# Expert weights stored in HBM in the order in which they are loaded

## The reference

```python
def expert_choice_ffn(x, router_w, wg, wu, wd):
    cap = CAPACITY_FACTOR * n // N_EXPERTS            # 32 tokens for each of 16 experts
    aff = softmax(einsum('bnd,de->bne', x, router_w))
    gate, idx = lax.top_k(aff.transpose(0, 2, 1), cap)
    xg = x[bidx, idx]
    hid = silu(einsum('becd,edf->becf', xg, wg)) * einsum('becd,edf->becf', xg, wu)
    o = einsum('becf,efd->becd', hid, wd) * gate[..., None]
    return zeros_like(x).at[bidx, idx].add(o)
```

## Time and profile before

| | |
|---|---|
| median of three runs | 2715.48 us (2713.36 to 2717.77) |
| span of the profiled execution | 2717.3 us |
| TensorE busy, granted clock (mean) | 2302.9 us (85%), 0.965 |
| VectorE, ScalarE busy | 1037.0 us (38%), 811.7 us (30%) |
| DMA | 660.17 MB, 243 GB/s over the span |
| chain that ended last | PE 57%, DMA 29%, DVE 7%, ACT 4% |

### The profile page before, as it was taken

One profiled execution on the slowest core, in us unless ns is written; L12 is line 12 of the kernel. 1 busy time (PEld: TensorE's weight loads), 2 busy tenths in 40 slices (PEclk: granted clock), 3 DMA queues, 4 the chain that ended last, 5 costly groups with the idle time before them and its releaser, 6 DMA issues.

```text
span 2717.3 us, 32508 instructions
## 1 busy us (share of the span) xinstructions
PE 2302.9 (85%) x13952; PEld 1613.8 (59%) x13952; DVE 1037.0 (38%) x1361; ACT 811.7 (30%) x989; POOL 67.6 (2%) x99
## 2 busy tenths in 40 slices
PE   5998888777777898787777778999999989988997
PEld 3855643222222585631111116999899989988997
DVE  4536451000000455510000004556855555556555
ACT  3425321000000344410000004432744354434433
POOL 0022000000000002000000000000000000000000
PEclk8999899999999998899999999999999999999998
DMA  7392357999999330389999995554355444452542
GB/s 264 109 385 107 120 220 280 409 409 410 410 410 410 143 131 6 118 323 409 409 410 410 410 410 204 179 180 175 123 186 186 167 149 165 181 186 93 186 165 72
DMA packets 205376, 660.17 MB, mean 243 GB/s; under 512 B 5632, under 2 KB 27136, under 8 KB 198624
## 3 DMA queue, kind: packets, MB, share of 16 engines
q1 hardware_dynamic: 204176, 653.67, 62.6%
q0 software_dynamic: 1104, 5.11, 0.5%
HBM read 657.71 MB, written 1.05 MB: 242 GB/s over the span
## 4 chain that ended last, share of the span: by engine, by line
PE 57%; DMA 29%; DVE 7%; ACT 4%; SPq 2%; issue 1%; POOL 0%; DVEq 0%; ACTq 0%; POOLq 0%
PE ps L694 13%; PE ps L695 13%; PE ps L696 13%; DMA ring<-in_exp_up 13%; DMA ring<-in_exp_gate 11%; PE ps L1011 6%; DMA ring<-in_w_in 2%; DVE ring_r L361 2%; PE ps L567 2%; SPq L453 2%; DMA ring<-in_ffn_gate 2%; ACT ring_r L354 1%; PE ps L833 1%; PE ps L1026 1%; PE ps L723 1%
## 5 line engine op out<-in xcount | busy, mean ns | idle before, releaser
L1011 PE MATMUL ps<-ring,arena 128*64 128x512 f32 (+1 forms) x2048 | 466.6, 600 | 165.1 <-DMA ring<-in_exp_up 81.9
L694 PE MATMUL ps<-h_buf_r,ring_r 128*128 128x256 f32 (+1 forms) x1856 | 540.8, 291 | 17.6 <-DVE h_buf_r L652 12.2
L696 PE MATMUL ps<-h_buf_r,ring_r 128*128 128x256 f32 (+1 forms) x1856 | 537.9, 290 | 0.0
L361 DVE TENSOR_TENSOR ring_r<-ring,ring_r 128x4096 fp32r<-128x4096 f32 (+2 forms) x97 | 406.2, 4192 | 304.6 <-ACT ring_r L354 304.6
L695 PE MATMUL ps<-h_buf_r,ring_r 128*128 128x256 f32 x1696 | 482.9, 285 | 0.0
L1011 PEld LDWEIGHTS ps<-ring,arena 128*64 128x64 f32 (+1 forms) x2048 | 128.2, 124 | 502.2 <-issue 295.3
L354 ACT ACTIVATE ring_r<-ring 128x4096 fp32r<-128x4096 f32 (+2 forms) x97 | 332.7, 3434 | 262.4 <-DMA ring<-in_ffn_down 107.6
L694 PEld LDWEIGHTS ps<-h_buf_r,ring_r 128*128 128x128 f32 x1856 | 360.4, 194 | 22.9 <-issue 16.7
L696 PEld LDWEIGHTS ps<-h_buf_r,ring_r 128*128 128x128 f32 x1856 | 360.2, 194 | 3.3
L695 PEld LDWEIGHTS ps<-h_buf_r,ring_r 128*128 128x128 f32 x1696 | 328.8, 194 | 0.2
L695 PE MATMUL ps<-arena_r,ring_r 128*128 128x256 f32 (+1 forms) x944 | 278.3, 295 | 0.0
(11 more groups left out here) (273 smaller groups left out, 2325.0 us busy)
## 6 DMA issues: line engine op xcount, KB each, us to landing
ring<-in_exp_gate SPq DMA_DIRECT2D x64, 2048.0 KB, 23.7
ring<-in_exp_up SPq DMA_DIRECT2D x64, 2048.0 KB, 23.8
ring<-in_exp_down SPq DMA_DIRECT2D x64, 2048.0 KB, 23.7
ring<-in_ada_w SPq DMA_DIRECT2D x24, 2048.0 KB, 14.7
ring<-in_ffn_gate SPq DMA_DIRECT2D x20, 2048.0 KB, 7.7
ring<-in_ffn_up SPq DMA_DIRECT2D x20, 2048.0 KB, 7.8
ring<-in_ffn_down SPq DMA_DIRECT2D x20, 2048.0 KB, 7.9
ring<-in_w_in SPq DMA_DIRECT2D x6, 2048.0 KB, 20.8
```

Of the source, the lines that this page charges most:

```text
L361: dve.tensor_tensor(rest, slot(n)[:, 0:halved[n]], lead, ALU.subtract).then_inc(sem("chunk_halved"), 1)
L694: release(pe.matmul(out, a[0], b[0], start=start, stop=False, skip_group_check=True))
L696: return pe.matmul(out, a[1], b[0], start=False, stop=stop, skip_group_check=True)
L1011: mm = pe.matmul(ps[half * m:half * m + m, which, :], xe[:, k, :], slot(n + c)[:, D * (k % 4) + 512 * half:D * (k % 4) + 512 * half + 512] ...
```

## The change

The host stores the three expert arrays as (layer, expert, half, partition, 4096 floats). One load is then one stretch of 2 MB in HBM and one partition's part of it one row of 16 KB. The load on SyncE becomes a plain copy of [128 x 4096]. The bytes that land in each partition of the slot, the number of loads, their order, their waits and all that reads the slots stay as they are.

```diff
@@ -449,8 +449,8 @@
                         sp.wait_ge(weights_used, it * 24 + (n + c - SLOTS + 1))
                         half = c % 2
-                        src = w[l, it * 4 + c // 6, half * 512:half * 512 + 512, :].rearrange("(k p) n -> p k n", p=P)
-                        sp.dma_start(slot(n + c).rearrange("p (k n) -> p k n", k=4), src)\
+                        src = w[l, it * 4 + c // 6, half, :, :]
+                        sp.dma_start(slot(n + c), src)\
                             .then_inc(slot_loaded[slot_of[n + c]], 16)
@@ -2310,6 +2310,10 @@
+    def by_partition(w):
+
+        return w.reshape(LAYERS, EXPERTS, 2, 4, P, -1).transpose(0, 1, 2, 4, 3, 5).reshape(LAYERS, EXPERTS, 2, P, SLOT)
+
@@ -2330,7 +2334,8 @@
-        "exp_gate": a["exp_w_gate"], "exp_up": a["exp_w_up"], "exp_down": a["exp_w_down"],
+        "exp_gate": by_partition(a["exp_w_gate"]), "exp_up": by_partition(a["exp_w_up"]),
+        "exp_down": by_partition(a["exp_w_down"]),
```

## The result

The kernel with the change ran at a median of **2676.7 us** (2671.1 to 2678.1, 4 runs) against 2716.1 us (2713.4 to 2717.8, 4 runs) for the kernel before: 39.4 us less, ratio 0.9849, 95% interval 0.9835 to 0.9863. The forecast was 2676 us, a range of 2669 to 2690.

The account below looks back on a forecast made before the run. DMA transfers were taken to bound the two expert stages, the only ones at a DMA limit. 180 loads at 0.22 us less each give 39.5 us, so the median 2715.5 us becomes 2676 us, range 2669 to 2690.

Parts of the forecast that it names:

- What bounds the kernel: Two expert stages: DMA transfers at 410 GB/s set the end of both; PE follows, needing 22.96 us an expert against 30.7.
- Which loads count: Expert stages: 90 of 96 loads in each layer, 180 in all; the first six are hidden behind the router.
- The prediction's check: Layer 0: first landing at 435.5 us plus 90 loads of 5.12 us plus one w_in load gives 901.7, against 903.3 us.
- What a load costs: Each expert load: 4.90 us with 16 KB rows against 5.12 now, 0.22 us less; 39.5 us in 180 loads.
- The straight line: Row price under a full queue: 150.9 ns per 4096 bytes plus 9.1 ns a row, so 612.7 ns at 16 KB.
- The rule of about 3 cycles a packet: Other price for expert loads' rows: an estimated 3.5 ns fixed overhead per packet, giving 15 us saved, not 39.5.
- The other parts of the edit: SyncE's issue, PE's chain between gate, up and down, instruction fetches and other engines' work: no cost found.
- landing near 22.8 us: Sign in the profile after: an expert load mid-stage takes near 22.8 us from issue to landing, against 23.8 before.
- Rows are not cut: Expert loads: the rival had 16 KB rows cut into 4 KB pieces at issue, nothing changing, 2715 us; chance 6%.
- Only a third of the price: Expert loads: rival that only a third of the 9.1 ns a row goes, 13 us saved, 2702 us; chance 4%.
- The place in HBM gives the gain: Expert loads: rival that most of the rate difference comes from where rows lie, not a fixed row price; 2702 us, chance 4%.
- The spacing slows HBM: Expert stages: rival that rows starting at multiples of 16 KB clash in memory, 54 us more, 2769 us; chance 5%.

Follow-up runs that it names:

- e1: The changed kernel with each partition's part of a load fetched as two rows of 8 KB instead of one of 16 KB; 2688.0 us, before 2717.3.
- e2: The changed kernel with each partition's part of a load fetched as eight rows of 2 KB; 2771.9 us, ratio 1.0207 to the kernel before.
- e3: The changed kernel with each partition's four 4 KB pieces one behind the other in HBM, 512-byte gaps keeping them separate rows; 2716.2 us, before 2717.3.
- e8: The kernel with the change run again, unaltered, beside other experiments; 2675.3 us, ratio 0.9850 to the kernel before.
- e4: The changed kernel with the 16 KB rows of a load 512 KB apart instead of adjacent; 2677.1 us, ratio 0.9855 to the kernel before.
- e10: The changed kernel with the 16 KB rows of a load 1 MB apart; 2671.7 us, ratio 0.9836 to the kernel before.
- e5: The changed kernel with all three expert arrays in one, the 16 KB rows of a load 4 MB apart; 3414.4 us, ratio 1.257 to the kernel before.

## Why the prediction was right, point by point

**What bounds the kernel** was read rightly, shown by e1, e2 and the change: a price of so many ns on each row moved the whole time by some 180 times what it did to a load, in both directions. What the reading of the chain left out is SyncE's held issue, 1.6% of it; e1 shows that it was no cost of its own.

**Which loads count**: 90 in each layer. By the measured rows a load takes 32 x 160.0 ns before and 8 x 612.0 ns after, 0.224 us less; 90 times that is 20.2 us, and the stretches in the table shrank by 20.2 and 20.3. All 96 would have given 21.5. The lengths alone don't settle it: e3, with rows of 4 KB, has stages of 482.2 and 477.4 us, 0.8 and 1.5 us more than before. What does is the DMA engines between PE's first expert matmul and the seventh load: 3 GB/s in both profiles (421.8 to 428 us before, 417.9 to 424 after), so the first six loads had landed and nothing waited for them.

The prediction's check, 901.7 us for w_in against 903.3, came so close by luck: 435.5 us is already the landing of the first of the 90, so 89 loads follow it, and the sum is 896.6. That is 6.7 us short, and counted the same way from 431.1 us the kernel after is 6.5 us short (872.6 for 879.1), so the gain is not touched.

**What a load costs.** Sum 39.5 us, stages 40.5 in the profiles, medians 39.4 in the first comparison and 41.4 in e8's. The term was a hair small: 612.0 ns and not 612.7. (The printed 160.0 ns would give 39.3 us; 39.5 comes from the unrounded 160.04.) That the median came within 0.7 us of 2676 is partly luck, since runs of one kernel spread over 4 to 7 us. The straight line was the right choice between the bounds of 27 and 45 us. The line held at 2 KB on contiguous loads too (e2), where it had been taken from `w_in` alone. What the runs show is the price of a row; whether it is paid in the engine or at the memory they don't show.

**The rule of about 3 cycles a packet** (the Trainium skill, "DMA: Bandwidth & Descriptors", section "Why small descriptors are slow (HBM only)") would have had an estimated 15 us; e1, e2 and the change each disagree with it by a factor of more than two.

**The other parts of the edit** cost nothing, as said. But of the signs that the prediction named one was wrong: landing near 22.8 us. The step that failed there is that it scaled the 23.8 us by the rate. A slot comes free when PE is done with a load, and six loads later its next load lands: some 6 x 4.90 us less PE's 3.7 to 4 us on a load, 25.5 us; e1 was forecast in this way, 26 us, and had 25.9. Before, the clock of that measure started late, since SyncE was still held in the issue ahead of it: at 1591.26 us PE was done with a load, and SyncE was held for 2.81 us more. That SyncE is now free changed no time (e1), which the prediction had right.

Another sign failed in the first profile: the other stages were to be equal within a microsecond or two, and two of them were 3.9 and 3.5 us shorter; the start of e3 and the end of e8, in the table's terms, show that neither is the change's gain. And from the seventh load's issue (427.6 and 423.8 us in layer 0) the stages are 20.3 us shorter, just past the 19 to 20 named.

**The rivals.** Rows are not cut (packets, page above). "Only a third of the price" falls to e1 and e2. "The place in HBM gives the gain" falls to e3 and e4. "The spacing slows HBM" is false at 16 KB, 512 KB and 1 MB (the change, e4, e10), and true at 4 MB (e5).

## What to carry to other kernels

Where a stage runs at a flat DMA rate, look at how long the rows are before taking that rate for the limit: the packet counts of a few windows with different row lengths give a price for a row and one for its bytes, and these two numbers forecast each new layout here to a tenth of a microsecond a load, except that of e5. What has to be contiguous is what one partition gets, not the load; and a layout that puts partitions a large power of two apart should be measured before it is used, as e5 shows. A gain per load counts only for loads that something waits for: here 180 of 192, since the first six of each layer had landed before PE began. A name that leaves the chain with a change need not have been its cause: SyncE's 43 us did, and were no gain.

## What was not expected of the hardware

- The rate doesn't fall with the distance of the rows: 428 GB/s at 512 KB and at 1 MB, 234 at 4 MB, 429 at 4 MB + 16 KB.
- SyncE's issue was held for some 5 us behind loads of 32 and of 64 rows an engine and took 0.33 to 0.37 us with 8 and 16. The limit is not a fixed count of rows: 149 rows' time from issue to landing at 4 KB, 233 at 2 KB. What it counts stays open.
- Beside slower transfers TensorE's granted clock was lower too: 0.80 of full speed in e5's window, with TensorE busy for 60% of it, where both stages before stand at 9 tenths or more. It still waited for loads for 232 of the 600 us, so the transfers were the bound there all the same.
